# Experts of up to 64 tokens: the unsplit 32-bit weights in two 64-column halves of the array, and a new order of work in the expert stage

## The chip, the cores and the metric

One core of a Trainium2 chip runs the whole program. The metric is the device time of one launch in microseconds (us). Matrix products run on TensorE (PE in the rows; PEld is its weight load), element-wise work on ScalarE (ACT) and VectorE (DVE), lists and indirect transfers are issued by GpSimd (POOL), weight loads by SyncE (SP).

## The reference

A residual block for 512 tokens of width 1024. Three mixers run on a normed input, their gated sum is added to the residual, and then a sparse expert layer follows, which is all that changes here:

```python
xt = xn.reshape(T, D)
logits = (xt @ router_w) + router_b
top_v, top_i = lax.top_k(logits, TOP_K)            # 4 of 32 experts
top_w = jax.nn.softmax(top_v, axis=-1)
h = lax.ragged_dot(xs, w_gate_up, group_sizes) + b_gate_up[e_sorted]   # 1024 -> 2 x 1024
gate, up = h[:, :D_FF], h[:, D_FF:]
gate = jnp.minimum(gate, SWIGLU_LIMIT)
up = jnp.clip(up, -SWIGLU_LIMIT, SWIGLU_LIMIT)
a = (up + 1.0) * (gate * jax.nn.sigmoid(SWIGLU_ALPHA * gate))
y = lax.ragged_dot(a, w_down, group_sizes) + b_down[e_sorted]
y = y * top_w...                                    # then summed back per token
```

All data are float32. Each expert has 12 MB of weights (gate, up and down, 1024x1024 each), so the 32 experts read 384 MB from memory.

## The kernel before

The program first runs the mixers and the routing (until about 1075 us) and then `stage_moe`, which this change rewrites. Routing sorts the experts by their number of tokens and seats them: seat 0, the even seats and seat 31 hold the 17 larger experts ("big", up to 128 tokens), the odd seats 1 to 29 the 15 experts of up to 64 tokens ("small"; NS = 64). The stage works through the seats in pairs, one small and one big, in a hardware loop (`Fori`) of 14 rounds with a 15th pair written out behind it, and seat 31 after that.

Weights come in units of 1 MB, twelve for an expert: positions 0 to 3 and 8 to 11 of gate and up, positions 4 to 7 of down. There are 12 buffers `RAW[pos]`; SP refills `RAW[pos]` for the next expert as soon as TensorE has used it (`s_use`), so SP runs 12 units ahead. The turn of seat n multiplies up and gate of expert n and, in between, down of expert n-1.

Precision: every weight unit is split in two. ScalarE writes the rounded value to a ring of six `HI` buffers (`hi`, L2252), VectorE writes the rest over the raw unit, `LO = RAW - HI` (`lo`, L2259), and the tokens are split in the same way (`XTh`, `XTl`; `aTh`, `aTl`). A big expert's unit is 12 products of 128x128 by 128x512 in the format fp32r: hi x hi, hi x lo, lo x hi (L2276 to L2278). A small expert has at most 64 tokens; its rounded tokens stand in columns 0 to 63 of the stationary operand and their rests in columns 64 to 127 (`low`, `high`), so that a unit takes 8 products (L2269, L2270). The two halves of the result then have to be added across partitions: ScalarE copies the bank to `fold` (`to_fold`, L2317) and TensorE multiplies it by a 128x64 matrix of two identities (`fold_down`, L2311), five times for a small expert; for the first half of down the adding is done by ScalarE, VectorE and GpSimd (`keep_rest` L2449, `add_rest` L2454, L2503).

The order on each engine is written out by hand, in 12 slots for a turn, and each engine takes its instructions in program order. In slot s ScalarE rounds the unit of slot s+5 and VectorE takes the rest of the unit of slot s+4 (`ahead`); the conversions of tokens and activations stand between them. `turn_x` (L2287, 8 transposes) turns the gathered tokens of the next expert, `turn_a` (L2360, 4 transposes for a half) the activations; `silu`, `swiglu`, `keep_a_hi`, `keep_a_lo`, `keep_x_hi`, `keep_x_lo` and `weigh` are one ScalarE or VectorE operation on a 128x512 bank each (two for `keep_x_hi`, `keep_x_lo`). A unit covers four depth tiles by 512 columns, so that the first 512 columns of gate and up are complete, and their activations can be worked on, while the second 512 are multiplied.

Of the kernel before, what the change touches and what calls it, by code (L numbers as in the profile page):

```python
# [35 lines left out]
P = 128  # L36
# [1565 lines left out]
def stage_mix(K, ctx):  # L1602
# [399 lines left out]
    def _(dve):  # L2002
# [166 lines left out]
        dve.wait_ge(s_ls, 1)  # L2169
        nc.vector.tensor_copy(into(2).bitcast(F32), K.banks[7][:, 0:NE]).then_inc(s_first, 1)  # L2170
# [8 lines left out]
def stage_moe(K, ctx):  # L2179
# [7 lines left out]
    um, sg = K.place("moe_um", HF, b0 + 8 * FF), K.place("moe_sg", HF, b0 + 8 * FF + 4 * HF)  # L2187
    fold, onto = K.place("moe_fold", HF, b0 + 8 * FF + 8 * HF), K.place("moe_onto", NS, b0 + 8 * FF + 12 * HF)
    aTh, aTl = K.place("moe_aTh", FF, b1, R32), K.place("moe_aTl", FF, b1 + 4 * FF, R32)
    XTh = [K.place("moe_XTh0", KT * P, b1 + 8 * FF, R32), K.rounded("moe_XTh1", K.y_daT, KT * P, 0)]  # L2190
    XTl = [K.place("moe_XTl0", KT * P, b1 + 12 * FF, R32), K.rounded("moe_XTl1", K.y_daT, KT * P, KT * P)]
    Xg, LG = K.moe_Xg, K.moe_LG
    sel = K.moe_sel
    h1 = K.h1.rearrange("p (t d) -> p t d", t=TT)
    LS, LO_list = (sb(n, [P, 4], I32) for n in ("LS", "LO"))
    Hb, Yb, Tb = K.banks[0:4], K.banks[4:6], K.banks[6:8]
    (s_hi, s_lo, s_use, s_LS, s_XT, s_XTh, s_XTl, s_sel, s_sg, s_cl, s_a, s_aT, s_aTh, s_aTl,
     s_ys, s_sc, s_LO, s_bd, s_h1, s_fk, s_fd, s_fc, s_yt, s_yw) = (K.sem("moe_" + n) for n in (
         "unit_hi", "unit_lo", "unit_used", "list_late", "XT", "XT_hi", "XT_lo", "bias_row",
         "silu", "up_clipped", "a", "aT", "aT_hi", "aT_lo", "y", "scattered", "over_list", "bias_down", "h1", "to_fold", "folded", "fold_const", "y_rest", "y_weighed"))  # L2200
    CAPPED = ALPHA * LIMIT / (1.0 + math.exp(-ALPHA * LIMIT))
    DOWN = range(4, 8)
    B = 12 * NE + 4
    ORDER = (0, 1, 2, 3, 8, 9, 10, 11, 4, 5, 6, 7)
    LAST = (6, 7, 4, 5)

    def count(n, pos):

        if isinstance(n, int) and n == 0:
            return pos + 5 if pos < 4 else pos + 1  # L2210
        if isinstance(n, int) and n == NE:
            return 12 * NE + LAST.index(pos) + 1
        return n * 12 + (pos + 1)

    def exists(n, pos):

        if isinstance(n, int) and n == 0:
            return pos not in DOWN
        if isinstance(n, int) and n == NE:
            return pos in DOWN  # L2220
        return True

    def ring(n, pos):

        if isinstance(n, int) and n == 0 and pos >= 8:
            return (4, 5, 2, 3)[pos - 8]
        return pos % 6
# [10 lines left out]
    def hi(act, n, pos):  # L2238

        if not exists(n, pos):  # L2240
            return
        act.wait_ge(s_w[pos], n * 16 if pos in DOWN else n * 16 + 16)
        if isinstance(n, int) and n == 0:
            if pos in (10, 11):
                act.wait_ge(s_use, count(0, pos - 8))
        elif isinstance(n, int) and n == 1 and pos in (2, 3):
            act.wait_ge(s_use, count(0, pos + 8))
        elif isinstance(n, int) and n == NE:
            act.wait_ge(s_use, count(n - 1, pos if pos >= 6 else pos + 6))
        else:  # L2250
            act.wait_ge(s_use, count(n, pos - 6) if pos >= 6 else count(n - 1, pos + 6))
        nc.scalar.activation(HI[ring(n, pos)][:], RAW[pos][:], ACT.Copy).then_inc(s_hi, 1)  # L2252

    def lo(dve, n, pos):

        if not exists(n, pos):
            return
        dve.wait_ge(s_hi, count(n, pos))
        nc.vector.tensor_tensor(LO[pos][:], RAW[pos][:], HI[ring(n, pos)][:].bitcast(F32),  # L2259
                                ALU.subtract).then_inc(s_lo, 1)  # L2260

    def unit(pe, done, pos, ring, bank, xh, xl, k0, start, stop, small=0):

        pe.wait_ge(s_lo, done)
        if small:
            for k in range(4):
                w = slice(k * HF, (k + 1) * HF)
                x = slice((k0 + k) * P, (k0 + k + 1) * P)
                nc.tensor.matmul(bank[:], xh[:, x], HI[ring][:, w], start=start and k == 0, stop=False)  # L2269
                mm = nc.tensor.matmul(bank[:], xh[:, x], LO[pos][:, w], start=False, stop=stop and k == 3)  # L2270
            mm.then_inc(s_use, 1)
            return
        for k in range(4):
            w = slice(k * HF, (k + 1) * HF)
            x = slice((k0 + k) * P, (k0 + k + 1) * P)
            nc.tensor.matmul(bank[:], xh[:, x], HI[ring][:, w], start=start and k == 0, stop=False)  # L2276
            nc.tensor.matmul(bank[:], xh[:, x], LO[pos][:, w], start=False, stop=False)  # L2277
            mm = nc.tensor.matmul(bank[:], xl[:, x], HI[ring][:, w], start=False, stop=stop and k == 3)  # L2278
        mm.then_inc(s_use, 1)

# [9 lines left out]
    def up_half(pe, n, par, j, half, place, small=0):  # L2290

        if j == 0 and half == 0:
            pe.wait_ge(s_XTl, n + 1)
            pe.wait_ge(s_sel, n + 1)
        if j % 2 == 0 and half == 0 and not (isinstance(n, int) and n == 0):
            pe.wait_ge(s_a, n * 2 + (j // 2 - 1))
        if half == 0:
            nc.tensor.matmul(Hb[j][:], sel[par][:], K.moe_bias[:, j * HF:(j + 1) * HF], start=True, stop=False)  # L2298
        done, pos, ring = place
        unit(pe, done, pos, ring, Hb[j], XTh[par], XTl[par], 4 * half, False, half == 1, small)  # L2300

    def up(pe, n, par, j, places):

        for half in range(2):
            up_half(pe, n, par, j, half, places[half])

    def fold_down(pe, f, bank):

        pe.wait_ge(s_fc, 1)
        pe.wait_ge(s_fk, f + 1)  # L2310
        nc.tensor.matmul(bank[0:NS, :], onto[:], fold[:], start=True, stop=True).then_inc(s_fd, 1)  # L2311

    def to_fold(act, f, bank, ready):

        act.wait_ge(s_use, ready)
        act.wait_ge(s_fd, f + 1)
        nc.scalar.activation(fold[:], bank[:], ACT.Copy).then_inc(s_fk, 1)  # L2317

    def places(n, at):

        return [(count(n, at + i), at + i, ring(n, at + i)) for i in range(2)]
# [16 lines left out]
    def first_half(pe):  # L2338

        done, pos, ring = count(0, 0), 0, 0  # L2340
        x, w = [slice(k * P, (k + 1) * P) for k in range(4)], [slice(k * HF, (k + 1) * HF) for k in range(4)]
        pe.wait_ge(s_sel, 1)
        nc.tensor.matmul(Hb[0][:], sel[0][:], K.moe_bias[:, 0:HF], start=True, stop=False)
        pe.wait_ge(s_lo, done)
        pe.wait_ge(s_XTh, 1)
        for k in range(4):
            nc.tensor.matmul(Hb[0][:], XTh[0][:, x[k]], HI[ring][:, w[k]], start=False, stop=False)  # L2347
        for k in range(4):
            nc.tensor.matmul(Hb[0][:], XTh[0][:, x[k]], LO[pos][:, w[k]], start=False, stop=False)
# [5 lines left out]
    def turn_a(pe, n, half):
        pe.wait_ge(s_a, n * 2 + (half + 1))
        if not (isinstance(n, int) and n == 0):
            pe.wait_ge(s_aTl, START + n * 2 + (half - 1))
        for k in range(4):
            mm = nc.tensor.transpose(Tb[half][:, k * P:(k + 1) * P], a[:, (4 * half + k) * P:(4 * half + k + 1) * P],  # L2360
                                     K.ident[:])
        mm.then_inc(s_aT, 1)

    def down(pe, n, kept, where):

        pe.wait_ge(s_aTl, START + n * 2 + 2)
        pe.wait_ge(s_XTl, kept)
        for j in range(2):
            for half in range(2):
                done, pos, ring = where[2 * j + half]  # L2370
                unit(pe, done, pos, ring, Yb[j], aTh, aTl, 4 * half, half == 0, half == 1)

    def low(t):

        return t.rearrange("p (k c) -> p k c", c=P)[:, :, 0:NS]

    def high(t):

        return t.rearrange("p (k c) -> p k c", c=P)[:, :, NS:P]

    def keep_x_hi(act, n, par, small=0):
        act.wait_ge(s_XT, n + 1)
# [669 lines left out]
```

## Time and profile before

| | |
|---|---|
| median of 3 runs | 2168.43 us (2166.55 to 2171.65) |
| span of the profiled execution | 2168.4 us |
| TensorE busy | 2111.0 us, 97% of the span |
| VectorE, ScalarE, GpSimd busy | 1564.6, 1318.4, 566.5 us |
| read from memory | 504.91 MB |
| expert stage | from 1075.7 us to the end |

The profiled execution's span and the median of the runs agree to 0.1 us, so times of the trace can be compared with the median as they are. The rows of a page or view give, for a group of instructions, the busy time, the mean duration of one in ns, and the idle time of the engine just before them with what ended it. Durations of matmuls overlap, since they are pipelined; what one costs is the distance between two starts. An fp32 matmul that is not fp32r stands in the trace as two instructions.

### The profile page before, as it was taken

The page shows a single profiled execution, that of the slowest core. Times are in us where ns is not written, and L with a number is a line of the kernel's source. Part 1 is how long each engine was busy: PE and PEld are TensorE (multiplying, and loading weights), DVE is VectorE, ACT ScalarE, POOL GpSimd, SP SyncE. Part 2 cuts the span into 40 slices and gives each one's busy share as a digit, 9 for nine tenths or more (in the row PEclk, how much of TensorE's full clock was granted, in tenths as well). Part 3 has the DMA queues.
Part 4 walks back from the last instruction along what each step waited for, and adds up shares of the span by engine and source line. Part 5 has one row for each costly group of instructions (what it writes and reads, how often), then busy time and mean ns, then how long its engine had stood idle before and what let it go on. Part 6 is the DMA issues. An engine that isn't in the chain of part 4 may idle for free.

```text
span 2168.4 us, 29886 instructions
## 1 busy us (share of the span) xinstructions
PE 2111.0 (97%) x9638; PEld 1652.6 (76%) x9638; DVE 1564.6 (72%) x1690; ACT 1318.4 (61%) x1606; POOL 566.5 (26%) x429
## 2 busy tenths in 40 slices
PE   6999899999999999999899999999999999999998
PEld 6888677776667888888767777777777777777776
DVE  6777454754444334434689999999999999999996
ACT  5566453334232433323468888888888888888884
POOL 3333100201232000000214234443244332343421
PEclk9999999999999999999799999999999999999999
DMA  5110232320112343435589999999999999999993
GB/s 193 59 58 29 98 117 78 133 78 30 49 40 88 97 136 97 136 96 165 204 325 376 405 391 391 405 391 401 392 391 399 397 385 402 388 393 399 393 395 120
DMA packets 87095, 516.01 MB, mean 238 GB/s; under 512 B 13124, under 2 KB 14148, under 8 KB 36264
## 3 DMA queue, kind: packets, MB, share of 16 engines
q1 hardware_dynamic: 79448, 498.30, 59.6%
q0 software_dynamic: 7296, 16.79, 3.2%
q8 instruction: 37, 0.61, 0.1%
q14 instruction: 26, 0.21, 0.0%
q10 hardware_dynamic: 288, 0.09, 0.0%
HBM read 504.91 MB, written 19.40 MB: 242 GB/s over the span
## 4 chain that ended last, share of the span: by engine, by line
PE 49%; DVE 1%; DMA 0%; ACT 0%; issue 0%; POOL 0%; POOLq 0%; DVEq 0%; ACTq 0%
PE bank L2276 9%; PE bank L2278 8%; PE bank L2277 8%; PE bank L2269 8%; PE bank L2270 8%; PE bank L2311 3%; PE bank L2298 1%; PE bank L2287 1%; PE bank L2360 1%; DVE moe_lo L2259 1%; DMA out<-y_daT 0%; PE bank L2347 0%; DVE y_daT L2336 0%; ACT moe_hi L2252 0%; PE bank L2352 0%
## 5 line engine op out<-in xcount | busy, mean ns | idle before, releaser
L2259 DVE TENSOR_TENSOR moe_lo<-moe_raw,moe_hi 128x2048 fp32r<-128x2048 f32 x382 | 857.1, 2286 | 7.1 <-ACT moe_hi L2252 5.4
L2252 ACT ACTIVATE moe_hi<-moe_raw 128x2048 fp32r<-128x2048 f32 x380 | 722.3, 1915 | 62.8 <-PE bank L2278 54.4
L173 ACT ACTIVATE unit_hi<-unit_raw 128x1024 fp32r<-128x1024 f32 x116 | 122.2, 1059 | 241.8 <-DMA unit_raw<-in_w_units 235.7
L179 DVE TENSOR_TENSOR unit_lo<-unit_raw,unit_hi 128x1024 fp32r<-128x1024 f32 x116 | 145.3, 1258 | 163.5 <-ACT unit_hi L173 163.1
L2276 PE MATMUL bank<-moe_hi,moe_XTh 128*128 128x512 f32 x540 | 215.9, 400 | 0.0
L2278 PE MATMUL bank<-moe_hi,moe_XTl 128*128 128x512 f32 x540 | 211.5, 392 | 0.0
L2277 PE MATMUL bank<-moe_lo,moe_XTh 128*128 128x512 f32 x540 | 211.0, 391 | 0.0
L2269 PE MATMUL bank<-moe_hi,moe_XTh 128*128 128x512 f32 x480 | 194.5, 405 | 2.8 <-DVE moe_lo L2259 2.8
L2270 PE MATMUL bank<-moe_lo,moe_XTh 128*128 128x512 f32 x480 | 190.8, 398 | 0.0
L2503 POOL TENSOR_SCALAR moe_y<-moe_y,moe_LS 64x512 f32<-64x512 f32 x15 | 93.2, 6213 | 324.3 <-ACT moe_y L2466 324.3
L2505 POOL DMA_INDIRECT out<-moe_y,moe_LS x32 | 117.8, 3680 | 229.5 <-ACT moe_y L2466 215.9
L2276 PEld LDWEIGHTS bank<-moe_hi,moe_XTh 128*128 128x128 f32 x540 | 101.6, 188 | 43.6 <-issue 24.3
L2269 PEld LDWEIGHTS bank<-moe_hi,moe_XTh 128*128 128x128 f32 x480 | 91.2, 190 | 46.5 <-DVE moe_lo L2259 14.9
L2278 PEld LDWEIGHTS bank<-moe_hi,moe_XTl 128*128 128x128 f32 x540 | 101.3, 188 | 22.6
L2277 PEld LDWEIGHTS bank<-moe_lo,moe_XTh 128*128 128x128 f32 x540 | 101.5, 188 | 20.8
L2276 PE MATMUL bank<-moe_hi,moe_aTh 128*128 128x512 f32 x272 | 107.8, 396 | 0.6 <-DVE moe_lo L2259 0.6
L2270 PEld LDWEIGHTS bank<-moe_lo,moe_XTh 128*128 128x128 f32 x480 | 91.1, 190 | 20.5
L2278 PE MATMUL bank<-moe_hi,moe_aTl 128*128 128x512 f32 x272 | 106.1, 390 | 0.0
L2277 PE MATMUL bank<-moe_lo,moe_aTh 128*128 128x512 f32 x272 | 105.9, 389 | 0.0
L1749 PE MATMUL bank<-yH,unit_hi 128*128 128x512 f32 x256 | 100.4, 392 | 2.0 <-DVE mix_da_lo L1640 2.0
L1751 PE MATMUL bank<-yH,unit_lo 128*128 128x512 f32 x256 | 100.5, 393 | 0.0
L393 PE MATMUL bank<-da_slab_hi,xnH 128*128 128x384 f32 x256 | 92.3, 361 | 5.3 <-DVE xnL L214 5.3
(411 smaller groups left out, 4486.1 us busy)
## 6 DMA issues: line engine op xcount, KB each, us to landing
moe_raw<-in_w_moe SPq DMA_DIRECT2D x384, 1024.0 KB, 8.4
unit_raw<-in_w_units SPq DMA_DIRECT2D x116, 512.0 KB, 3.6
da_slab<-in_w_qkv SPq DMA_DIRECT2D x8, 1536.0 KB, 6.8
y_caT<-in_x SPq DMA_DIRECT2D x4, 512.0 KB, 5.8
yda_d<-y_daT SPq DMA_DIRECT2D x1, 2048.0 KB, 6.3
y_daT<-in_blocks_qk SPq DMA_DIRECT2D x1, 2048.0 KB, 10.9
y_daT<-yda_d SPq DMA_DIRECT2D x1, 2048.0 KB, 7.9
y_daT<-in_x SPq DMA_DIRECT2D x1, 2048.0 KB, 8.6
```

What stands on the lines that cost most here:

```text
L173: K.nc.scalar.activation(K.whi[:, i, :], K.wraw[:, i, :], ACT.Copy).then_inc(K.s_whi, 1)
L179: K.nc.vector.tensor_tensor(K.wlo[:, i, :], K.wraw[:, i, :], K.whi[:, i, :].bitcast(F32), ALU.subtract).then_inc(K.s_wlo, 1)
L1749: nc.tensor.matmul(bank[:], whi[:, i, w], hi[:, x], start=(k0 + k == 0), stop=False)
L1751: mm = nc.tensor.matmul(bank[:], wl, hi[:, x], start=False, stop=(k0 + k == depth - 1))
L2252: nc.scalar.activation(HI[ring(n, pos)][:], RAW[pos][:], ACT.Copy).then_inc(s_hi, 1)
L2259: nc.vector.tensor_tensor(LO[pos][:], RAW[pos][:], HI[ring(n, pos)][:].bitcast(F32), ALU.subtract).then_inc(s_lo, 1)
L2269: nc.tensor.matmul(bank[:], xh[:, x], HI[ring][:, w], start=start and k == 0, stop=False)
L2270: mm = nc.tensor.matmul(bank[:], xh[:, x], LO[pos][:, w], start=False, stop=stop and k == 3)
L2276: nc.tensor.matmul(bank[:], xh[:, x], HI[ring][:, w], start=start and k == 0, stop=False)
L2277: nc.tensor.matmul(bank[:], xh[:, x], LO[pos][:, w], start=False, stop=False)
L2278: mm = nc.tensor.matmul(bank[:], xl[:, x], HI[ring][:, w], start=False, stop=stop and k == 3)
L2505: nc.gpsimd.indirect_dma_start(A["out"], bass.IndirectOffsetOnAxis(ap=LS[0:rows, 0:1], axis=0), y[0:rows, :], None, bounds_check=S - 1, oo ...
```

## The change

A small expert's weights are no longer split. TensorE multiplies the 32-bit unit `RAW[pos]` as it landed, as true fp32, with 64 stationary columns (`XTs`, `aTs`). A unit now covers two depth tiles by all 1024 columns; for a small expert the first 512 columns go to the array's columns 0 to 63 and the second 512 to columns 64 to 127 (`half(bank, j)`), so both halves of a result lie in one bank, on partitions 0 to 63 and 64 to 127. Rounding, rests, folds, `keep_rest` and `add_rest` of small experts go. Of a small expert's activation the four transposes of one call turn both halves. The order of the units changes for all experts: first the four units of up, then the four of down of the expert before, then the four of gate; the clipping of up stands behind up, silu and swiglu behind gate. The order of ScalarE's and VectorE's work around the units is written anew.

```diff
+    def unit(pe, h, ring, pos, banks, xh, xl, k0, start, stop, step=1):
+        pe.wait_ge(s_lo, h + 1)
+        for kk in range(2):
+            x = slice((k0 + kk) * P, (k0 + kk + 1) * P)
+            for j in range(2):
+                w = cut(kk, j)
+                nc.tensor.matmul(banks[j][:], xh[:, x], HI[ring][:, w], start=start and kk == 0, stop=False)
+                nc.tensor.matmul(banks[j][:], xh[:, x], LO[pos][:, w], start=False, stop=False)
+                mm = nc.tensor.matmul(banks[j][:], xl[:, x], HI[ring][:, w], start=False, stop=stop and kk == 1)
+        mm.then_inc(s_use, step)
+    def small_unit(pe, pos, arrived, bank, xs, k0, start, stop):
+        pe.wait_ge(s_w[pos], arrived)
+        for kk in range(2):
+            for j in range(2):
+                mm = nc.tensor.matmul(half(bank, j), xs(k0 + kk), RAW[pos][:, cut(kk, j)], start=start and kk == 0,
+                                      stop=stop and kk == 1)
         mm.then_inc(s_use, 1)
+    def small_bias(par, bank, j0):
+        for j in range(2):
+            nc.tensor.matmul(half(bank, j), sel[par][:, 0:NS].bitcast(F32),
+                             K.moe_bias[:, (j0 + j) * HF:(j0 + j + 1) * HF].bitcast(F32), start=True, stop=False)
...
+    def keep_a_small(act, n):
+        act.wait_ge(s_aT, START + n * 2 + 2)
+        act.wait_ge(s_use, n * 12 + 8)
+        nc.scalar.activation(aTs[:], Tb[0][:], ACT.Copy, scale=1.0 / ALPHA).then_inc(s_aTl, 2)
+    def weigh_ready(act, n):
+        act.wait_ge(s_use, count(n + 1, 7))
...
TensorE:
+            def small(n, it):
+                up_ready(pe, n)
+                small_bias(1, UP[0], 0)
+                for p in small_part(n, 0, UP[0]):
+                    if p == 1:
+                        turn_a(pe, n - 1, 0)
+                        turn_a(pe, n - 1, 1)
+                for p in range(4):
+                    if p % 2 == 0:
+                        down_ready(pe, n - 1, p // 2)
+                    unit(pe, nth(it, 8 + p), (8 + p) % 6, 4 + p, Yb, aTh, aTl, 2 * p, p == 0, p == 3)
+                gate_ready(pe, n)
+                small_bias(1, GATE[0], 2)
+                for p in small_part(n, 8, GATE[0]):
+                    if p == 1:
+                        turn_x(pe, n + 1)
+            def big(n, b, last):
+                up_ready(pe, n)
+                bias(0, UP, 0)
+                for p in big_part(n, b, 0, UP, 0):
+                    if p == 1:
+                        turn_a(pe, n - 1, 0, 2)
+                down_ready(pe, n - 1, 1)
+                for p in range(4):
+                    small_unit(pe, 4 + p, n * 16, Yb[0], xs_down, 2 * p, p == 0, p == 3)
+                gate_ready(pe, n)
+                bias(0, GATE, 2)
+                for p in big_part(n, b, 4, GATE, 0):
+                    if p == 1:
+                        turn_x(pe, n + 1)
...
ScalarE:
+            def small(n, it):
+                for h in range(2):
+                    silu(act, n - 1, h)
+                big_hi(act, n - 1, 8)
+                for h in range(2):
+                    keep_a_hi(act, n - 1, h)
+                for off in (9, 10, 11):
+                    big_hi(act, n - 1, off)
+                weigh(act, n - 1)
+                keep_x_hi(act, n + 1, 0)
+                for off in (0, 1):
+                    big_hi(act, n + 1, off)
+            def big(n, b, last):
+                silu(act, n - 1, 0, 2)
+                keep_a_small(act, n - 1)
+                for off in (2, 3, 4, 5):
+                    big_hi(act, n, off)
+                weigh_small(act, n - 1)
+                big_hi(act, n, 6)
+                if last:
+                    keep_x_hi(act, n + 1, 1)
+                else:
+                    keep_x_small(act, n + 1)
+                big_hi(act, n, 7)
...
VectorE:
+            def small(n, it):
+                for h in range(2):
+                    swiglu(dve, n - 1, h)
+                big_lo(dve, it, 8)
+                for h in range(2):
+                    keep_a_lo(dve, it, h)
+                clip(dve, n, 0, 2)
+                for off in (9, 10, 11):
+                    big_lo(dve, it, off)
+                keep_x_lo(dve, it + 1, 0)
+                for off in (0, 1):
+                    big_lo(dve, it + 1, off)
+            def big(n, b, last):
+                swiglu(dve, n - 1, 0, 2)
+                for off in (2, 3, 4):
+                    big_lo(dve, b, off)
+                for h in range(2):
+                    clip(dve, n, h)
+                for off in (5, 6):
+                    big_lo(dve, b, off)
+                if last:
+                    keep_x_lo(dve, b + 1, 1)
+                big_lo(dve, b, 7)
...
GpSimd, late():
-        if small:
-            nc.gpsimd.tensor_scalar(y[0:NS, 0:512], y[0:NS, 0:512], LS[0:NS, 2:3].bitcast(F32), None, ALU.mult).then_inc(s_yw, 1)
-            hold(K, pool, s_yw, w)
...
Routing (VectorE):
         dve.wait_ge(s_ls, 1)
+        for j in range(2):
+            nc.vector.tensor_copy(K.first[j * NS:(j + 1) * NS, :, 3].bitcast(F32), K.banks[7][0:NS, 0:NE])
```

Here `off` counts the twelve units of a big expert in the order in which TensorE uses them: 0 to 3 up, 4 to 7 gate (positions 8 to 11), 8 to 11 down (positions 4 to 7); `HI[off % 6]` is its ring buffer. Seat 31 at the end has an order of its own (`end`): up, down of seat 30, gate, and then its own down, each engine in that order; the activations of seat 31 can only begin when all four gate units are done. In it ScalarE rounds the fourth unit of up behind `keep_a_hi` of seat 30, VectorE takes the rests of the fourth and of the last units behind `keep_a_lo`, and both columns' `weigh` stand behind the last unit.

## Rows read from the trace of the kernel before

**Rows 1.** The page: busy time of the engines, and the 40 slices.

```profile
PE 2111.0 (97%) x9638; PEld 1652.6 (76%) x9638; DVE 1564.6 (72%) x1690; ACT 1318.4 (61%) x1606; POOL 566.5 (26%) x429
...
PE   6999899999999999999899999999999999999998
...
DMA  5110232320112343435589999999999999999993
```

**Rows 2.** Timeline of TensorE: the transposes of tokens for a big expert.

```profile
1142.50 1.04 PE L2287 MATMUL bank<-ident,moe_Xg 128*128 128x128 f32 x8
...
1508.44 1.03 PE L2287 MATMUL bank<-ident,moe_Xg 128*128 128x128 f32 x8
...
1574.87 1.03 PE L2287 MATMUL bank<-ident,moe_Xg 128*128 128x128 f32 x8
...
2072.55 1.03 PE L2287 MATMUL bank<-ident,moe_Xg 128*128 128x128 f32 x8
```

**Rows 3.** Busy time by stretch: one pair of experts (columns as named).

```profile
core 0: us, PE busy (x) PEld busy (x) DVE busy (x) ACT busy (x) POOL busy (x), PEclk, DMA share, GB/s
...
1508.60:1575.00 66.40, 66.40 (x293) 50.32 (x291) 62.75 (x42) 55.20 (x45) 25.66 (x13) 1.00 1.01 394
```

**Rows 4.** Loads of weights: issue to landing in one pair, and in the last 61 us.

```profile
DMA to landing us min/median/max: 5.8/8.6/11.6
...
DMA to landing us min/median/max: 4.8/4.9/8.1
```

**Rows 5.** Timeline of TensorE, one pair: a small expert's products, transposes, bias, a fold.

```profile
1515.24 0.40 PE L2269 MATMUL bank<-moe_hi,moe_XTh 128*128 128x512 f32 x1
...
1518.97 0.60 PE L2360 MATMUL bank<-ident,moe_a 128*128 128x128 f32 x4
1519.32 0.48 PE L2298 MATMUL bank<-moe_bias,moe_sel 128*128 128x512 f32 x1
1519.64 0.39 PE L2269 MATMUL bank<-moe_hi,moe_XTh 128*128 128x512 f32 x1
...
1521.27 0.40 PE L2270 MATMUL bank<-moe_lo,moe_XTh 128*128 128x512 f32 x1
1521.60 1.07 PE L2311 MATMUL bank<-moe_fold,moe_onto 128*64 128x512 f32 x2
1522.60 0.50 PE L2269 MATMUL bank<-moe_hi,moe_XTh 128*128 128x512 f32 x1
1522.93 0.39 PE L2270 MATMUL bank<-moe_lo,moe_XTh 128*128 128x512 f32 x1
```

**Rows 6.** Timeline of TensorE: fp32 products side by side, from another stage.

```profile
412.53 0.62 PE L1213 MATMUL bank<-ml_xm,ml_third 128*32 128x512 f32 x1
412.54 0.62 PE L1213 MATMUL bank<-xcT,ml_third 128*32 128x512 f32 x1
...
413.86 0.59 PE L1213 MATMUL bank<-xcT,ml_third 128*32 128x512 f32 x1
414.38 3.84 PE L1228 MATMUL bank<-ml_second,ml_xm 128*128 128x128 f32 x32
```

**Rows 7.** Groups by line and shape in the expert stage: duration of one.

```profile
L2252 ACT ACTIVATE moe_hi<-moe_raw 128x2048 fp32r<-128x2048 f32 x24 | 45.6, 1914 | 3.3 <-PE bank L2278 3.0 <-PE bank L2270 0.2
...
L2259 DVE TENSOR_TENSOR moe_lo<-moe_raw,moe_hi 128x2048 fp32r<-128x2048 f32 x25 | 56.1, 2286 | 0.0
```

**Rows 8.** Timeline of ScalarE, and of all engines at the end.

```profile
1542.24 1.09 ACT L2389 ACTIVATE moe_XTh<-bank 128x512 fp32r<-128x512 f32 x2 [0.28 <-PE bank L2287]
...
2150.76 0.60 PE L2360 MATMUL bank<-ident,moe_a 128*128 128x128 f32 x4
2151.39 0.60 ACT L2432 ACTIVATE moe_aTh<-bank 128x512 fp32r<-128x512 f32 x1 [1.18 <-PE bank L2360]
```

**Rows 9.** Busy time, granted clock and DMA share by stretch, behind two waits.

```profile
1107.90:1110.70 2.80, 0.01 (x1) 1.00 1.00 418
1112.00:1115.30 3.30, 3.30 (x9) 0.50 0.97 390
1115.40:1118.70 3.30, 0.84 (x4) 1.00 0.92 367
1118.80:1122.10 3.30, 3.30 (x10) 0.50 0.53 221
```

**Rows 10.** Timeline of TensorE, the start of the stage: the two waits.

```profile
1107.49 0.40 PE L2298 MATMUL bank<-moe_bias,moe_sel 128*128 128x512 f32 x1
1110.69 0.50 PE L2269 MATMUL bank<-moe_hi,moe_XTh 128*128 128x512 f32 x1 [2.80 <-DVE moe_lo L2259]
...
1118.72 1.09 PE L2360 MATMUL bank<-ident,moe_a 128*128 128x128 f32 x4 [2.48 <-DVE moe_a L2423]
```

More of the change, by code:

```diff
@@ L2288, in turn_x, with up_ready, gate_ready @@
         mm.then_inc(s_XT, 1)
[L2290 to L2321, printed above, removed]
+    def up_ready(pe, n):
+        pe.wait_ge(s_XTl, n + 1)
+        pe.wait_ge(s_sel, n + 1)
+        if not (isinstance(n, int) and n == 0):
+            pe.wait_ge(s_cl, n * 2)
+    def gate_ready(pe, n):
+        if not (isinstance(n, int) and n == 0):
+            pe.wait_ge(s_sg, n * 2)
     def bias_down(pe, t):
@@ L2355, in turn_a @@
[L2355 to L2360, printed above, removed]
-                                     K.ident[:])
[L2362 to L2381, printed above, removed]
+        x = [slice(k * P, (k + 1) * P) for k in range(2)]
+        for w in (HI[0], LO[0]):
+            for kk in range(2):
+                for j in range(2):
+                    nc.tensor.matmul(UP[j][:], XTh[0][:, x[kk]], w[:, cut(kk, j)], start=False, stop=False)
+        pe.wait_ge(s_XTl, 1)
@@ L2515, in overflow, with pairs @@
                 body(i, NE + i)
-    def pair(it, turn, last=0):
-        turn(it * 2 + 1, 1, True, 1, 0, 0, it * 5)
-        turn(it * 2 + 2, 0, True, 0, 1, 1 - last, None, it * 5, it)
+    def pairs(eng, small, big):
+        with eng.Fori(0, PAIRS - 1) as it:
+            small(it * 2 + 1, it)
+            big(it * 2 + 2, it + 1, False)
+        small(NE - 3, PAIRS - 1)
+        big(NE - 2, PAIRS, True)
     with nc.Block(no_gpsimd_drain=True) as block:
@@ L2624, in item @@
+            turn_x(pe, 0)
+            first_unit(pe)
+            for t in range(TT):
+                bias_down(pe, t)
+                if t < TT - 1:
+                    unit(pe, t + 1, t + 1, t + 1, UP, XTh[0], XTl[0], 2 * (t + 1), False, t == 2, 5 if t == 2 else 1)
+            turn_x(pe, 1)
+            bias(0, GATE, 2)
+            for p in big_part(0, 0, 4, GATE, 0):
+                pass
+            pairs(pe, small, big)
+            end()
             def item(i, n):
-                spot = [(i * 12 + (B + q + 1), p, q % 6) for q, p in enumerate(ORDER)]
+                base = SPLITS + i * 12
@@ L2632, in _ @@
+                for h in range(2):
+                    turn_a(pe, n, h)
+                down_ready(pe, n, 1)
+                for p in range(4):
+                    unit(pe, base + (8 + p), (8 + p) % 6, 4 + p, Yb, aTh, aTl, 2 * p, p == 0, p == 3)
             overflow(pe, item)
@@ L2698, in _ @@
-            with act.Fori(0, PAIRS - 1) as it:
-                pair(it, turn)
-            pair(PAIRS - 1, turn, 1)
-            turn(NE - 1, 1, False)
-            hi(act, NE, 4)
-            hi(act, NE, 5)
-            keep_a_hi(act, NE - 1, 1, NE * 12 - 4)
-            weigh(act, NE - 1, 1, 12 * NE + 3)
-            weigh(act, NE - 1, 0, 12 * NE + 4)
+            keep_x_small(act, 1)
+            pairs(act, small, big)
+            end()
             def item(i, n):
```

625 lines of the change are left out of this document (278 added, 347 removed).

## The prediction

> **What bounds the kernel now.** The page comes first: TensorE is busy 97% of the span, and in the second half the DMA engines are busy too [rows 1]. So the expert stage has two candidates. The tokens of a big expert are turned once in every pair, at 1508.44 and again at 1574.87: a pair takes 66.43 us, and from 1142.50 to 2072.55 there are 14 such pairs, 66.43 each [rows 2]. Inside a pair TensorE has no idle time at all, VectorE works 62.8 of 66.4 us, ScalarE 55.2, and the DMA share is 1.01 at 394 GB/s [rows 3]. The landings tell which of the two waits for the other. A load takes 4.8 us when nothing is queued (the least of the last loads), and inside a pair between 5.8 and 11.6 us with a median of 8.6 [rows 4]. The queue is thus never empty, yet it is short: twelve buffers are refilled in turn, one unit is used in 66.43/24 = 2.77 us, so a load has 33 us and needs 8.6. TensorE sets the pace, and the DMA engines have next to nothing in reserve. The reader is to keep both: work taken from TensorE is worth something only down to about 66 us a pair, and a wait put before TensorE costs in full.
>
> **What the change takes from TensorE, for a pair.** A small expert's 96 products go. Their distance is 0.233 us (16 from 1515.24 to 1518.97 [rows 5]); with down a little faster, 22.2 us. Five folds go, each 1.00 us from start to the next start and 0.1 at each side where its neighbours stand further apart [rows 5]: 6.0. Four biases at 0.23, 0.9; four transposes at 0.35 and 0.09 behind them [rows 5], 0.4. From 66.4 this leaves 36.9.
>
> **What it adds to TensorE.** 24 pairs of fp32 products for the weights and 2 for the biases. The trace has no such pair with 64 columns, but it has 32-column ones: eight products, of two instructions each, begin at 412.53, and the next work starts at 414.38 [rows 6]. That is four at a time, 0.44 us for an instruction. Were two halves to overlap as well, a pair of products takes 2 x 0.437 = 0.87 us, and 26 take 22.7; if they didn't, 26 x 1.75 = 45.4. I take the first, since the rows are of the same kind. For going into fp32 with half the array and back, five or six times, I take the 0.2 us seen around a fold, 1.2 in all (bounds 0 and 3). TensorE's own work is then 36.9 + 22.7 + 1.2 = 60.8 us a pair.
>
> The Trainium skill, TensorEngine Tiling (Array Packing), Key Properties, says that changing the tiling mode drains TensorE. By the row around the fold that is 0.2 us and no more; priced by a whole isolated fold instead, six changes would be some 6 us and not 1.2.
>
> The same skill, DMA: Bandwidth & Descriptors, Specifications, puts the fabric's ceiling at 435 GB/s; 26.4 MB a pair would need 60.7 us by it. This trace moves 394 GB/s with the engines at 1.01, so the measured floor of a pair stays about 66.
>
> **What the new order puts before TensorE.** ScalarE and VectorE have 12 units to convert instead of 24, so by sums they have time: 23 + 5 and 27 + 6 us of 66. But each takes its instructions in order, and the conversions that depend on a transpose now stand ahead of units that TensorE wants next. Durations: hi 1.91, lo 2.29 [rows 7]; two token copies 1.09; from the start of four transposes to ScalarE's copy 0.63, the copy 0.60 [rows 8]; a big unit 12 x 0.229 = 2.75; a small unit 1.75; eight transposes 0.8 to pass, 1.03 to be done [rows 2]. I count from the start of `turn_x` for the big expert, which is 0.
>
> Hold 1: ScalarE rounds units 0 and 1 only behind `keep_x_hi`. Copies done at 2.2, hi 4.15, lo 6.45. TensorE would be ready at 5.05 (transposes 0.9, two small units 3.5, biases and switch 0.65). It stands for 1.4.
>
> Hold 2, the largest: units 0 and 1 run to 12.0. `turn_a` for the small expert follows, `keep_a_small` waits for it, and `big_hi(2)` stands behind `keep_a_small`. Transposes done 12.7, copy 13.3, hi 15.2, lo 17.5. TensorE has been free since 12.5: 5.0. Units 2 and 3 end at 23.0, four small down units at 30.2, the biases at 30.8, units 4 and 5 at 36.3.
>
> Hold 3: `big_hi(7)` stands behind `keep_x_small`, which waits for `turn_x`: 37.4, copies (256 columns each) 38.1, hi 40.0, lo 42.3. TensorE is through unit 6 at 40.0: 2.3. Unit 7 ends at 45.1.
>
> Then the small bias and two units to 49.6, both `turn_a` 1.0, two units 3.5; the second down unit is 0.4 late, since VectorE's clip waits for the end of up and stands before its lo; four down units 11.0, bias 1.0, two units 3.5, switches 0.1: 70.0. Check: 60.8 of work and 9.1 of holds, 69.9. The DMA engines need 66 of that and are out of the way.
>
> **The clock.** Two waits at the start of the stage, 2.80 and 2.48 us [rows 10], were each followed by 3.3 us and more at half the granted clock with TensorE busy throughout [rows 9]; that loses 1.7 us each. Hold 2 is twice as long, so I put 1.9 on it; hold 3, just under those two, I price at 1.7 in six cases of ten, hold 1 at one in ten. Together 3.1. A pair: 73.1 us, 6.7 more than before; 14 pairs, +93.4.
>
> **Start and end.** The small expert in seat 1 needs no rounding, so both waits of [rows 10] go. From the end of gate of seat 0 (1107.0, one `turn_a` less than before) it is bias and two units 4.5, `turn_a` 1.0, two units 3.5, down 11.4, bias and two units 4.5: `turn_x` at 1132.0 instead of 1142.5 [rows 2], -10.5. Behind 2072.55 the kernel before needs 95.9 us. The new one has the same big units, no folds, 45.6 to the end of seat 30 with hold 3 at 2.8, and then seat 31: up with the fourth unit 2.4 late, one down unit 1.2 late, gate to 84.2; silu and swiglu 1.6; ScalarE rounds another unit before it copies the turned half, VectorE likewise, 4.3; the third down unit 2.2 late, last product at 104.3. Then 8.7 (before 8.0, one `weigh` more), and 6.6 for half clock behind four or five of these holds: 119.6, +23.7. Two more copies in the routing at under 0.2 us each: +0.4. GpSimd loses 6.2 us of work a pair, which hid beside TensorE: 0. SP's queue keeps its order: 0.
>
> Sum: 2168.4 - 10.5 + 93.4 + 23.7 + 0.4 = 2275. A change within 0.2% (4.3 us) can't be told from none.
>
> **Rivals.**
> (B) The holds come but the clock stays up. Pairs 70.0: 2168.4 - 10.5 + 14 x 3.6 + 17 + 0.4 = 2226. For it: other gaps of under 2 us; against it: the two of [rows 9].
> (C) The other side. The holds vanish, because ScalarE's order is not what I read or the chains overlap more; then the DMA engines bound a pair at 66.4 as now. TensorE follows its loads more closely at the end (it trails by 33 - 8.6 = 24.6 us now, with rounding and queue at some 11 it gains 13), 6 us of DMA idling at the start are used, and the end's holds cost 4: about 2153. It decides at 5.6 us of holds a pair, the difference of 66.4 and 60.8: below that nothing of them shows. Hold 2 alone is near it, so (C) needs hold 2 to be absent.
> (D) The halves don't run at once, or 7 us of 64-column products let the clock fall: 22.7 us more a pair, 2168 - 6 + 14 x 29 + 46 = 2615. Against it: [rows 6].
> (E) The holds are partly hidden, a pair stays at 66.4: 2168, no change. It needs holds cut by half and nothing gained at the ends.
>
> **Chances.** Forecast 0.66 (its own range 2235 to 2310), B 0.15, C 0.10, D 0.07, E 0.02. Leaving out C, E and D, and the outer edge of B, the range is 2208 to 2312. Faster 0.10, same 0.01, slower 0.89.
>
> **What would show it.** Right: `turn_x` for big experts 70 to 75 us apart; TensorE idle about 5 us before the third up unit of every big expert, ended by lo; 2.3 us before its last gate unit; granted clock near 0.93; DMA share near 0.92; landings shorter than 8 us. Two matmuls of 128x64 starting within 0.02 us of each other, next pair 0.44 later. Wrong: unit 2's hi starting before `turn_a` ends; DMA share still 1.0 and TensorE waiting for landings (C); 64-column products 0.44 apart one by one (D).

## The result, and the profile after

The changed kernel takes 2281.0 us, the median of 4 runs (2279.3 to 2283.7). The kernel before takes 2167.5 beside it (2165.5 to 2171.7). The ratio is 1.0523, with a 95% interval of 1.0508 to 1.0538: slower by 5.2%. The profiled execution has a span of 2282.1 us, 113.7 more than the 2168.4 of before.

The page of the changed kernel, the same lines as [rows 1]:

```profile
PE 2089.6 (92%) x9488; PEld 1487.5 (65%) x9488; DVE 1121.6 (49%) x1406; ACT 947.4 (42%) x1334; POOL 300.8 (13%) x398
...
PE   7999899999999999998988889888988889888986
...
DMA  4110332311113424254999999899999898898962
```

Every engine has less to do than before: VectorE 443 us less, ScalarE 371. And yet it is slower. Many of TensorE's 9s have become 8s in the expert stage, and so have some of the DMA engines'. When neither TensorE nor the DMA engines are full throughout, one waits for the other in turn. TensorE's timeline gives the length of a pair, as [rows 2] did:

```profile
1132.68 1.09 PE L2336 MATMUL bank<-ident,moe_Xg 128*128 128x128 f32 x8
...
1206.17 1.09 PE L2336 MATMUL bank<-ident,moe_Xg 128*128 128x128 f32 x8
...
1278.98 1.09 PE L2336 MATMUL bank<-ident,moe_Xg 128*128 128x128 f32 x8
...
2159.39 1.09 PE L2336 MATMUL bank<-ident,moe_Xg 128*128 128x128 f32 x8
```

These are 14 pairs in 1026.71 us, 73.34 each, where [rows 2] have 66.43. So the 113.7 us split into three parts: 9.8 less before the first of these rows (1132.68 against 1142.50), 14 x 6.91 = 96.7 more in the pairs, and 26.8 more behind the last (122.7 against 95.9).

Who is waited for, in the view of waits of TensorE from 1090 us to the end (total us, times, the longest):

```profile
PE bank L2292 <- DVE moe_lo L2240: 134.1, 64, 4.9
PE bank L2292 <- issue: 3.8, 1, 3.8
PE bank L2389 <- DVE moe_a L2443: 1.5, 1, 1.5
```

There is practically one kind of wait: a split product that waits for the low part of its weights. TensorE's timeline shows where in a pair it stands (the bracket is the idle time ahead of the row):

```profile
1212.66 0.50 PE L2292 MATMUL bank<-moe_hi,moe_XTh 128*128 128x512 f32 x1 [1.15 <-DVE moe_lo L2240]
...
1218.24 0.60 PE L2389 MATMUL bank<-ident,moe_a 128*128 128x128 f32 x4
1223.70 0.80 PE L2292 MATMUL bank<-moe_hi,moe_XTh 128*128 128x512 f32 x1 [4.86 <-DVE moe_lo L2240]
...
1250.88 0.50 PE L2292 MATMUL bank<-moe_hi,moe_XTh 128*128 128x512 f32 x1 [2.20 <-DVE moe_lo L2240]
...
1266.11 0.50 PE L2292 MATMUL bank<-moe_hi,moe_aTh 128*128 128x512 f32 x1 [0.22 <-DVE moe_lo L2240]
```

Those are the first, third and eighth unit of the big expert and the second of its down product: 8.43 us. The first three are the prediction's holds 1, 2 and 3. The chain behind the 4.86 is read from the timelines of ScalarE and, in the second fence, VectorE:

```profile
1218.92 0.60 ACT L2462 ACTIVATE moe_aTs<-bank 128x512 f32<-128x512 f32 x1 [6.36 <-issue]
1219.42 7.30 ACT L2235 ACTIVATE moe_hi<-moe_raw 128x2048 fp32r<-128x2048 f32 x4
...
1246.04 0.66 ACT L2417 ACTIVATE moe_XTs<-bank 128x256 f32<-128x256 f32 x2 [3.65 <-PE bank L2336]
1246.58 1.92 ACT L2235 ACTIVATE moe_hi<-moe_raw 128x2048 fp32r<-128x2048 f32 x1
```

```profile
1221.35 6.69 DVE L2240 TENSOR_TENSOR moe_lo<-moe_raw,moe_hi 128x2048 fp32r<-128x2048 f32 x3 [5.91 <-ACT moe_hi L2235]
```

ScalarE stands idle for 6.36 us, while TensorE works through units 0 and 1. It does so only because the next instruction in its order is the copy of the turned half. When TensorE has turned it (1218.24), the copy runs, then the rounding that TensorE by now is waiting for, then VectorE's part, and at 1223.70 TensorE goes on. The second pair of rows of ScalarE (1246.04 and 1246.58) is the same at unit 7.

The granted clock, by stretch (columns: busy us of PE, PEld, DVE, ACT, POOL, then PEclk, DMA share, GB/s):

```profile
1132.68:1206.17 73.49, 65.07 (x282) 39.30 (x281) 33.27 (x22) 30.66 (x27) 7.80 (x10) 0.95 0.95 364
...
1174.32:1176.52 2.20, 0.00 (x1) 0.00 (x1) 2.14 (x1) 0.00 (x0) 0.00 (x0) 1.00 1.01 423
1177.84:1181.25 3.41, 3.41 (x10) 2.16 (x10) 0.00 (x0) 0.23 (x1) 0.10 (x1) 0.50 1.00 416
...
1222.21:1229.04 6.83, 5.34 (x13) 4.18 (x14) 5.84 (x3) 4.51 (x3) 0.00 (x0) 0.50 0.48 202
```

Half clock (0.50, the level of 1.2 GHz) holds for 3.41 us behind the 2.20 us gap and for 6.83 us around the end of the 4.86 us gap, 5.34 of them with TensorE at work. Counted over the 14 pairs, hold 2 is followed by it every time, hold 3 in 7 of 14 (in every second pair), hold 1 never; half of TensorE's busy time in those stretches is 3.25 us a pair. The small expert's four down units have this row in the same view, of their line alone:

```profile
1231.83:1238.85 7.02, 7.02 (x32) 2.21 (x32) 1.00 0.99 393
```

That is 0.219 us for an instruction of 128x64 at full clock, 0.439 for two. And the loads of the pair from 1206 us land faster than those of [rows 4], in the median; the least is the 4.7 us of a load with next to nothing ahead of it:

```profile
DMA to landing us min/median/max: 4.7/7.4/12.1
```

### The profile page after: what moved, and what is told of

The parts are those of the page before. It is cut to its first block, busy times and chain, and to the rows that moved or that the text cites. A ratio compares the mean times of both kernels' runs of the same rounds, so it can differ in the third digit from the quotient of the medians.

```text
span 2282.1 us, 28033 instructions
## 1 busy us (share of the span) xinstructions
PE 2089.6 (92%) x9488; PEld 1487.5 (65%) x9488; DVE 1121.6 (49%) x1406; ACT 947.4 (42%) x1334; POOL 300.8 (13%) x398
## 4 chain that ended last, share of the span: by engine, by line
PE 32%; ACT 7%; DVE 7%; issue 6%; ACTq 0%; POOL 0%; POOLq 0%
PE bank L2306 9%; PE bank L2292 7%; DVE moe_lo L2240 7%; ACT moe_hi L2235 6%; PE bank L2294 6%; PE bank L2293 6%; PE bank L2327 1%; PE bank L2336 1%; PE bank L2389 0%; PE bank L2322 0%; ACT moe_XTh L2402 0%; ACT moe_XTs L2417 0%; ACTq L2234 0%; DVE moe_um L2433 0%; ACT moe_aTh L2450 0%
## 5 line engine op out<-in xcount | busy, mean ns | idle before, releaser
L2240 DVE TENSOR_TENSOR moe_lo<-moe_raw,moe_hi 128x2048 fp32r<-128x2048 f32 x202 | 455.5, 2290 | 278.4 <-ACT moe_hi L2235 221.6
L2235 ACT ACTIVATE moe_hi<-moe_raw 128x2048 fp32r<-128x2048 f32 x200 | 371.4, 1911 | 6.5 <-PEq L136 2.6
L2292 PE MATMUL bank<-moe_hi,moe_XTh 128*128 128x512 f32 x540 | 236.2, 437 | 128.1 <-DVE moe_lo L2240 128.1
L2293 PE MATMUL bank<-moe_lo,moe_XTh 128*128 128x512 f32 x540 | 227.2, 421 | 0.0
L2292 PEld LDWEIGHTS bank<-moe_hi,moe_XTh 128*128 128x128 f32 x540 | 111.5, 206 | 168.9 <-DVE moe_lo L2240 145.9
L2306 PE MATMUL bank<-moe_raw,moe_XTs 128*64 128x512 f32 x960 | 217.7, 595 | 0.0
L2514 POOL DMA_INDIRECT out<-moe_y,moe_LS x32 | 49.3, 1541 | 772.3 <-ACT moe_y L2475 389.2
L2306 PEld LDWEIGHTS bank<-moe_raw,moe_XTs 128*64 128x64 f32 x960 | 66.1, 137 | 126.4 <-issue 126.4
L2294 PEld LDWEIGHTS bank<-moe_hi,moe_XTl 128*128 128x128 f32 x540 | 111.1, 206 | 26.2
L2293 PEld LDWEIGHTS bank<-moe_lo,moe_XTh 128*128 128x128 f32 x540 | 112.6, 209 | 23.1
L2306 PE MATMUL bank<-moe_raw,moe_aTs 128*64 128x512 f32 x480 | 106.3, 595 | 0.0
```

The costliest lines, as they stand in the source:

```text
L2235: nc.scalar.activation(HI[ring][:], RAW[pos][:], ACT.Copy).then_inc(s_hi, 1)
L2240: nc.vector.tensor_tensor(LO[pos][:], RAW[pos][:], HI[ring][:].bitcast(F32), ALU.subtract).then_inc(s_lo, 1)
L2292: nc.tensor.matmul(banks[j][:], xh[:, x], HI[ring][:, w], start=start and kk == 0, stop=False)
L2293: nc.tensor.matmul(banks[j][:], xh[:, x], LO[pos][:, w], start=False, stop=False)
L2294: mm = nc.tensor.matmul(banks[j][:], xl[:, x], HI[ring][:, w], start=False, stop=stop and kk == 1)
L2306: mm = nc.tensor.matmul(half(bank, j), xs(k0 + kk), RAW[pos][:, cut(kk, j)], start=start and kk == 0, stop=stop and kk == 1)
```

## The experiments

All times are medians; a ratio is against the kernel before, run on the same chip. Beside the runs that undo the holds, one by one and all together, the kernel before took 2170.3 us, beside the others 2169.3.

**One hold at a time.** Hold 2, in ScalarE's order:

```diff
                 silu(act, n - 1, 0, 2)
+                for off in (2, 3):
+                    big_hi(act, n, off)
                 keep_a_small(act, n - 1)
-                for off in (2, 3, 4, 5):
+                for off in (4, 5):
                     big_hi(act, n, off)
```

> Undoes hold 2 alone: ScalarE rounds units 2 and 3 of a big expert ahead of keep_a_small and not behind it. My theory (the hold is the order of ScalarE, and it alone brings the half clock behind it): the 4.86 us before the third up unit vanish and with them about 2.35 us of clock, a pair would be 73.34 - 7.2 = 66.1 of TensorE's own pace, so the DMA engines become its bound at 66.4: 15 x 6.9 = 104 us less, about 2177. Rival B (no clock price): 15 x 4.9 = 73 us less, 2208. Rival 'something else holds unit 2' (its load, or VectorE's clip and swiglu): a new wait of 2 us or more stands in the same place and the time is above 2230.

Measured: 2167.0 us, ratio 0.9986 (0.9975 to 0.9996). This one move gives back 114 us. TensorE's timeline in a big expert:

```profile
1138.87 0.50 PE L2292 MATMUL bank<-moe_hi,moe_XTh 128*128 128x512 f32 x1 [1.15 <-DVE moe_lo L2240]
...
1144.45 0.60 PE L2389 MATMUL bank<-ident,moe_a 128*128 128x128 f32 x4
1144.80 0.48 PE L2292 MATMUL bank<-moe_hi,moe_XTh 128*128 128x512 f32 x1
```

The third unit follows the transposes at once; hold 1 is still there. A pair takes 65.54 us on average, 65.1 to 65.2 where no half clock falls in it (11 of 14). I had set a floor of 66.4 by the DMA engines, and this is below it; that is why 2177 was too much. The loads say how: issue to landing from 1132 to 1330 us, and from 1850 to 2050.

```profile
DMA to landing us min/median/max: 7.3/10.1/14.4
...
DMA to landing us min/median/max: 13.2/16.0/19.6
```

The queue grows, so the loads do not keep this pace; TensorE lives on the lead that they had. Half clock follows hold 3 in only 3 of the 14 pairs now.

Hold 3 (in ScalarE's order; in the last pair VectorE's low part of unit 7 moves ahead of that of the tokens likewise):

```diff
-                big_hi(act, n, 6)
+                for off in (6, 7):
+                    big_hi(act, n, off)
                 if last:
                     keep_x_hi(act, n + 1, 1)
                 else:
                     keep_x_small(act, n + 1)
-                big_hi(act, n, 7)
```

> Undoes hold 3 alone: ScalarE rounds unit 7 ahead of the copy of the turned tokens, in all 15 big experts. My theory: 2.20 us a pair and half of 1.6 us of clock go, 3.0 in all, 15 x 3.0 = 45 us less: 2236. Rival (a short hold costs no clock): 33 us less, 2248. Rival (the copy of the tokens, now 1.9 us later, delays the small expert's gate units or hold 2 grows by as much): no gain, 2281.

Measured: 2231.3 us, ratio 1.0286 (1.0267 to 1.0304), a pair 69.99: 3.35 less, of which 2.20 are the gap.

Hold 1:

```diff
# ScalarE, small()
-                keep_x_hi(act, n + 1, 0)
                 for off in (0, 1):
                     big_hi(act, n + 1, off)
+                keep_x_hi(act, n + 1, 0)
# VectorE, small()
+                big_lo(dve, it + 1, 0)
                 keep_x_lo(dve, it + 1, 0)
-                for off in (0, 1):
-                    big_lo(dve, it + 1, off)
+                big_lo(dve, it + 1, 1)
```

> Undoes hold 1 alone: units 0 and 1 of the next big expert are rounded ahead of its tokens' copy. My theory: 1.15 us a pair and no clock, 15 x 1.15 = 17 us less: 2264. Rival (the tokens' own copies, now later, hold the same units): 2275 or more. Rival (this short gap has a clock price as well, 1.7): 43 us less, 2238.

Measured: 2257.2 us, ratio 1.0411 (1.0390 to 1.0432), a pair 71.61: 1.73 less, where the gap is 1.15. In this kernel no half clock is left behind hold 3, though hold 3 is still 2.20 us long; so the removal of one gap also changes what follows another. In exchange the half clock behind hold 2 falls on more work, 5.1 to 5.9 us of it; by the same count as above the clock costs 2.9 us a pair and not 3.25. That is most of what the run gained beyond the 2264 expected.

**All three together**, the end as it was.

> All three holds undone, the end left as it is. My theory: TensorE's own work is 62.0 us a pair (70.2 at full clock less 8.2 of holds), so the DMA engines bound a pair at 66.4 and TensorE waits for loads: 14 x 6.9 = 97 less, 11 less in seat 30, and up to 13 for TensorE following its loads more closely: 2160 to 2175, 2168 taken; DMA share 1.0. Rival (no DMA bound; TensorE runs at its own 62): 14 x 4.4 less again, about 2110. Rival (a new hold in the order takes the place of the three): pairs above 68, over 2195.

Measured: 2157.6 us, ratio 0.9951 (0.9934 to 0.9968), less than the 2160 to 2175 expected. This is the run that shows both bounds. By stretch (columns as above): the first two pairs, and 139 us near the end.

```profile
1128.98:1190.29 61.31, 61.09 (x282) 37.42 (x281) 33.26 (x23) 30.77 (x28) 8.56 (x10) 1.00 1.02 406
1190.29:1251.61 61.32, 61.10 (x283) 37.43 (x281) 33.18 (x23) 30.68 (x28) 8.58 (x10) 1.00 1.02 406
1900.00:2039.22 139.22, 131.65 (x597) 78.56 (x595) 65.98 (x44) 64.02 (x56) 23.63 (x21) 1.00 1.00 397
```

For two pairs TensorE runs at its own pace, 61.3 us with 0.2 idle. The third takes 64.0, and the other eleven 65.5 to 66.1, mean 65.8, at a DMA share of 1.00. ScalarE's timeline there shows what the rounding waits for, and the landings from 1500 to 1700 us how far behind the queue is:

```profile
1514.24 1.92 ACT L2235 ACTIVATE moe_hi<-moe_raw 128x2048 fp32r<-128x2048 f32 x1 [0.48 <-DMA moe_raw<-in_w_moe]
...
1535.70 1.91 ACT L2235 ACTIVATE moe_hi<-moe_raw 128x2048 fp32r<-128x2048 f32 x1 [9.89 <-DMA moe_raw<-in_w_moe]
```

```profile
DMA to landing us min/median/max: 21.0/24.1/27.5
```

TensorE has used up a lead of (65.8 - 61.3) x 2 + 1.8 = 10.8 us, and from there the DMA engines set the pair. The 66.4 was too high as their floor. The lead also explains the run with hold 2 undone: at 65.2 to 65.5 it loses 0.3 to 0.6 us a pair to the loads, 8 us at most over 14 pairs, so its lead lasts.

**The clock by itself.** Hold 2 stays, but TensorE is kept at work in it:

```diff
                         turn_a(pe, n - 1, 0, 2)
+                        for _ in range(20):
+                            nc.tensor.matmul(Yb[1][:], XTh[0][:, 0:P], K.moe_bias[:, 0:512], start=True, stop=True)
```

> The changed kernel with its three holds, and 20 more products of the 128x512 kind, into a bank that nobody reads then, put before the third up unit of every big expert: 20 x 0.229 = 4.6 us of the 4.86 of hold 2, so that TensorE is busy while it is held. They do work that the result does not use. My theory (half clock follows the idle time): hold 2 keeps its length, but its 6.83 us of half clock go, 2.35 us a pair or more: 15 x 2.35 = 35 less, 2246; by the run with hold 2 undone (its pair 65.54 and 4.86 on top, 70.4) 2240. Rival (the half clock has another cause, such as the change from 32-bit products to split ones): 2281, and the rows of half clock stay where they are.

Measured: 2259.5 us, ratio 1.0412 (1.0390 to 1.0435): 21.5 us less than the changed kernel, where 35 were expected. By stretch, hold 2 with the filler, the unit behind it, then hold 3 and what follows it:

```profile
1501.74:1506.80 5.06, 4.83 (x23) 3.65 (x21) 2.29 (x2) 4.73 (x4) 0.00 (x0) 1.00 1.02 424
1506.86:1512.60 5.74, 5.74 (x26) 4.46 (x26) 4.34 (x2) 3.02 (x2) 0.00 (x0) 1.00 0.50 177
1529.41:1531.61 2.20, 0.00 (x1) 0.00 (x1) 2.15 (x1) 0.00 (x0) 0.00 (x0) 0.99 1.01 423
1531.61:1535.00 3.39, 3.39 (x8) 2.71 (x9) 0.00 (x0) 0.00 (x0) 0.00 (x0) 0.50 1.03 428
```

The cause is as I said: without the idle time the units behind hold 2 run at 1.00, and not at 0.50. The sum was not: hold 3 is now followed by half clock in 11 of 14 pairs and not in 7, which takes back 4 x 1.7 / 14 = 0.5 us a pair (71.58 measured, 71.0 expected): 8 of the 13 us by which 2246 was missed. Behind the last pair the time is 123.3 us and not 2.35 under the 122.7 of the changed kernel, 3 us more than expected: there half clock follows two more of the gaps, those of 2.07 and 2.21 us. The other 2 are within the spread of the runs (2254.2 to 2260.8). In the run with hold 1 undone, the one with hold 2 undone, the changed kernel and this run, the same 2.20 us gap brings half clock in 0, 3, 7 and 11 of 14 pairs. What decides it was not settled.

**The halves.** Both 64-column products of a step, and those of the bias, go to the same columns and to different banks, so that they can't overlap by their columns:

```diff
+    def apart(bank, j):
+
+        at = [b is bank for b in K.banks].index(True)
+        return K.banks[at + j][0:NS, :]
...
-                mm = nc.tensor.matmul(half(bank, j), xs(k0 + kk), RAW[pos][:, cut(kk, j)], start=start and kk == 0,
+                mm = nc.tensor.matmul(apart(bank, j), xs(k0 + kk), RAW[pos][:, cut(kk, j)], start=start and kk == 0,
...
-            nc.tensor.matmul(half(bank, j), sel[par][:, 0:NS].bitcast(F32),
+            nc.tensor.matmul(apart(bank, j), sel[par][:, 0:NS].bitcast(F32),
```

> The changed kernel with the two 64-column products of every step in the same columns of the array and two different banks, so that they cannot run at once. The second half of each small expert's values is then not used: its output rows are not the reference's. My theory (the halves overlap only because they use different columns): 26 pairs of products cost 2 x 0.86 and not 0.86, 22.3 us a pair more, less 1.4 for hold 1 and the short hold in down, which hide behind the longer small units: pair 94, 15 x 21 = 315 more: about 2597. Rival (overlap does not come from the columns): no change, 2281.

Measured, one run: 2589.5 us; a pair takes 93.84. The four down units of a small expert, of their line alone, against the 7.02 us above:

```profile
1169.66:1183.05 13.39, 13.39 (x32) 4.11 (x30) 1.00 0.87 323
```

It is 0.418 us an instruction against 0.219. The banks change along with the columns; that they bring the difference is unlikely, since a big expert's products alternate between two banks too and start 0.23 us apart, but it was not tested by itself. The use of both halves is worth 20.5 us a pair, and the clock stays at 1.00 in these products either way. The Trainium skill, TensorEngine Tiling (Array Packing), Overview, gives up to 2x for 64 columns; this is 13.39 / 7.02 = 1.91.

**The bound of the loads.** On top of all three holds undone, half of the small experts' weight products are left out, while all loads stay:

```diff
-        for kk in range(2):
+        for kk in (1,):
...
-                mm = nc.tensor.matmul(half(bank, j), xs(k0 + kk), RAW[pos][:, cut(kk, j)], start=start and kk == 0,
+                mm = nc.tensor.matmul(half(bank, j), xs(k0 + kk), RAW[pos][:, cut(kk, j)], start=start,
```

> All three holds undone, and half of the small experts' weight products left out (the first of the two rows of blocks in every unit); loads are the same. The small experts' results are not the reference's. My theory (with the holds undone, the DMA engines set the pair at 65.8): the pair stays at 65.5 to 65.9 although TensorE has 10.3 us less work a pair; only the ends get shorter: 2145 to 2158. Rival (TensorE or the order sets 65.8): pair 55 to 60, 2157 - 14 x 8 = 2045 or less.

Measured: 2158.7 us, ratio 0.9949 (0.9932 to 0.9965), the same as with all products. By stretch, the 13 pairs behind the first, and TensorE's waits:

```profile
1184.80:2042.56 857.76, 725.94 (x3018) 483.87 (x3016) 428.35 (x286) 405.74 (x350) 136.16 (x131) 0.92 1.01 400
```

```profile
PE bank L2322 <- DVE moe_XTl L2408: 51.1, 14, 4.6
PE bank L2292 <- DVE moe_lo L2240: 45.4, 22, 3.9
PE bank L2292 <- DVE moe_aTl L2455: 36.3, 14, 3.4
```

The pairs take 857.76 / 13 = 65.98 us on average (64.2 to 68.9), though the first, with the lead of the loads still there, took 54.57. The 12 x 0.875 = 10.5 us of work taken away come back as waits: the loads are the bound at 65.8 to 66.0. The waits are put down to VectorE, which stands behind ScalarE, and ScalarE's largest wait, from 1300 to 2000 us, is for the loads:

```profile
ACT moe_hi L2235 <- DMA moe_raw<-in_w_moe: 134.3, 79, 8.6
```

**The end, and the version that the runs point to.** All three holds undone, and in `end` the same rule: what depends on a transpose or on a finished product stands behind the roundings that TensorE wants first.

```diff
# ScalarE, end(); VectorE likewise, with the clip of up behind unit 11
-                end_hi(act, 2)
+                for i in (2, 3):
+                    end_hi(act, i)
                 for h in range(2):
                     keep_a_hi(act, n - 1, h)
-                for i in range(3, 9):
+                for i in range(4, 12):
                     end_hi(act, i)
                 weigh(act, n - 1)
-                for i in range(9, 13):
+                for i in range(12, 16):
                     end_hi(act, i)
                 for h in range(2):
                     silu(act, n, h)
-                end_hi(act, 13)
                 for h in range(2):
                     keep_a_hi(act, n, h)
-                for i in (14, 15):
-                    end_hi(act, i)
                 weigh(act, n)
```

> All three holds undone, and in the last seat the copies that depend on a transpose or on the down product (turned halves, weighing) stand behind the roundings that TensorE wants first. My theory (the six waits of the end, 12.6 us, are holds of the same kind, of which silu, swiglu, turn and copy of the last gate must stay, 3.4, and 3 us of half clock go with them): 2157.6 - 9.2 - 3 = 2145. Rival (the last down units' loads or VectorE's sum of 16 roundings hold the end instead): 2153 or more.

Measured: 2144.6 us (2142.1 to 2147.5), ratio 0.9887 (0.9868 to 0.9907): it beats the kernel before by 1.1%, and the changed one by 6.0% (2144.6 / 2281.0). TensorE's waits from 2072 us on:

```profile
PE bank L2389 <- DVE moe_a L2443: 2.7, 1, 2.7
PE bank L2292 <- issue: 1.5, 1, 1.5
```

Of six waits, 12.6 us, two are left: silu and swiglu of the last expert, then its turn and copy. That no order removes these two is argued, not tested. Against the kernel before, the span is 25.2 us shorter (2143.2): 11.3 less before the first pair (1131.2), 14 x 1.45 = 20.3 less in the pairs, and 6.4 more behind the last.

## Why the prediction was right

Forecast 2275 (2208 to 2312), measured 2281.0; slower, as forecast.

**TensorE's own work of a pair**, 60.8 forecast. With the holds gone it is 61.1 (busy, first pairs of the run with all three undone). A pair of products, one for each half, was put at 0.87 us; the four down units hold eight such pairs, and 7.02 / 8 = 0.88. The step from 32-column to 64-column products [rows 6] was the right one, and the run with the halves apart shows its price had it failed, 2589.5, near the 2615 of rival D. Going into 64-column products and back widens the distance of starts by about 0.1 us each way (1253.51 to 1253.83 is 0.32 and not 0.23), somewhat less than the 0.2 around a fold that the term took.

**The holds**, 1.4, 5.0, 2.3 and 0.4 forecast; 1.15, 4.86, 2.20 and 0.22 measured, each in its place and each ended by lo. Each of the first three goes when ScalarE's one instruction is moved (for hold 1 VectorE's was moved along with it), so their cause is shown, not argued. The fourth, 0.22 us, was left where it is. The pair without clock was to be 70.0; it is 73.34 - 3.25 = 70.1.

**The clock**, 3.1 forecast, 3.25 measured. The split was a little different: hold 2 costs some 2.4 and not 1.9, hold 3 about 0.85 and not 1.0, hold 1 nothing and not 0.2, so that two errors cancel in part. That hold 3 came out at 7 of 14, next to the forecast's six in ten, is luck: the same gap gave anything from 0 to 11 in the variants. That idle time is the cause is shown by the filler. That the prices can simply be added is refuted: undone alone, the holds give 7.80 (hold 2), 3.35 and 1.73 us a pair, 12.9 together, more than the 11.7 of gaps and clock that there were.

**The start**, -10.5 and +0.4 forecast, -9.8 measured. The stage's first row starts 1.8 us later (1077.54 against 1075.73). Of this 1.7 are there before the routing's added copies (its row of `rt_off` starts at 1073.07, before at 1071.36), so the copies cost 0.1. The 1.7 lie within the spread between executions: in the nine traces with the changed routing, which have the same program up to there, that row starts anywhere from 1069.4 to 1074.9. Counted from the stage's own start, the gain is 11.6.

**The end**, +23.7 forecast, +26.8 measured. Here one hold was overlooked: `weigh` of seat 30 stands ahead of the rounding of the second gate unit of seat 31, and TensorE waits 2.21 us for it. The description of `end` ahead of the prediction leaves this `weigh` out, too. The others were foreseen within 0.5 (2.07 for 2.4, 0.83 for 1.2, 3.82 for 4.3, 2.16 for 2.2), and half clock took 7.8 and not 6.6.

**What would show it.** Clock 0.94 and DMA share 0.93 over the 14 pairs, for 0.93 and 0.92; landings at 7.4 and not 8.6.

**The rivals.** B: the clock does fall. D: the halves do overlap. E: the holds are not hidden. C, the one on the other side, has its mechanism confirmed by the run without holds: then the loads bound the pair. It was mis-sized twice, and the two errors cancel in part, so that its number is in part luck: the floor is 65.8 and not 66.4, since [rows 3] show a DMA share of 1.01 at a pace that TensorE set, so that the row held no floor but only an upper bound of it (the prediction's 26.4 MB a pair are 26.2 by the same row, 394 GB/s x 66.4 us, and nothing in its sum rests on them); and the end kept more than 4 us of holds. It gave 2153, and 2157.6 were measured. Its point of decision moves down to 65.8 - 61.3 = 4.5 us of idle time and clock a pair. The run with hold 2 undone, 2167.0, stands just on the other side of it.

**Where the gain went.** The change takes 5.1 us of 66.4 from TensorE. At most 0.6 of it can show in a pair, because the loads then set the pace; the rest of what the best version gains, it gains at the start and from the lead of 10.8 us. The order of ScalarE turned these few us into a loss of 6.9.

## What to carry to other kernels

When a helper engine gets less to do, look at its order before its sum: an instruction that waits for the engine that sets the pace must not stand ahead of one that this engine will wait for (ScalarE was 42% busy here and cost 5%). When the engine that sets the pace is relieved, ask first how far the next bound is: a DMA share of 1.0 with short landings (8.6 us) is a queue that just keeps up, one with long landings (24 us) is the bound itself.

## What the runs showed of the hardware

Half clock is not a price per gap. The same idle time of 2.20 us at the same place was followed by 3.41 us of half clock in 7 of 14 pairs, and with another gap of the pair removed or filled in 0, 3 or 11 of 14; idle time of 1.15 us never was. Shorter gaps than 2.20 can be followed by it too: in the pairs of the run with all three holds undone, two waits for a rounding held up by the loads, of 1.64 and 1.84 us, were, and nine others of 1.4 to 1.8 us were not. Gaps of 4.86 us always were, for 3.41 or 6.83 us; in the changed kernel the long stretches begin while the gap still lasts (1222.21, with the gap from 1218.84 to 1223.70), so that 4.2 to 5.5 us of them fall on work.

64-column fp32 products in the two column halves, 0.219 us apart at 1.00 of clock, did not lower the granted clock: in the first two pairs of the run with all holds undone it stays at 1.00 throughout. Nor did they one by one at 0.418 (1.00 in the row from 1169.66).
